# Index stage and even in-projection of a sparse-attention decoder put into one block, with the 256 best keys found by bisection

## The reference, cut to what matters

```python
def indexer_select(qi, wi, ki, qpos, topk):
    s = relu(einsum('bthd,bsd->bths', qi, ki))           # 8 heads of 64
    score = einsum('bths,bth->bts', s, wi)
    score = where(arange(L) <= qpos, score, -inf)
    _, idx = top_k(score, topk)                          # 256 of 1024; 136 of 544
...
def even_mixer(h, pos, R0, w_in, w_out, q_gain, k_gain, attend):
    qr, kr, vr, gr, qa, ka, va, qi, ki, wi = split(h @ w_in)
    ret, R = retention_branch(qr, kr, vr, gr, pos, R0)   # gate: silu(gr)
    qa, ka = rmsnorm(qa, q_gain), rmsnorm(ka, k_gain)
    att = attend(qa, ka, va, qi, ki, wi)
    return concatenate([ret, att], -1) @ w_out, R, ka, va, ki
```

## Time and profile before

| | |
|---|---|
| median of 3 runs | 3370.16 us (3369.79 to 3370.91) |
| span of the profiled execution | 3368.8 us |
| PE busy | 2930.4 us, 87% of the span |
| DVE busy | 1501.6 us, 45% |
| ACT busy | 683.3 us, 20% |
| POOL busy | 377.4 us, 11% |
| index stage, first to last | 65.15 to 278.9 us |
| even projection, to the next block | 278.9 to 646.8 us |

### The profile page before, as it was taken

How to read it: one execution, slowest core, us unless ns; L and a number is a source line. 1 busy time by engine, 2 the same in 40 slices (tenths; PEclk the granted TensorE clock), 3 DMA queues, 4 the chain that set the end, 5 groups by cost and what they waited for, 6 DMA issues and landing times. The chain is left out here.

```text
span 3368.8 us, 38811 instructions
## 1 busy us (share of the span) xinstructions
PE 2930.4 (87%) x16567; PEld 2680.5 (80%) x16567; DVE 1501.6 (45%) x2009; ACT 683.3 (20%) x1091; POOL 377.4 (11%) x352
## 2 busy tenths in 40 slices
PE   3397999772687989999999979977788999999998
PEld 3285777562563989999999979955488999999997
DVE  4058999477541342323323253436534323233233
ACT  2042111024331121111111122222132111111110
POOL 3602112250213010000000000005101000000000
PEclk6598999885798989999999989976698999999999
DMA  4002222304214121121211111100011111211111
GB/s 147 25 7 72 93 92 72 135 33 161 76 40 128 60 60 42 40 55 39 57 38 38 44 24 44 46 15 18 29 51 44 51 44 38 57 38 54 41 38 64
DMA packets 207072, 189.49 MB, mean 56 GB/s; under 512 B 18220, under 2 KB 159664, under 8 KB 206762
## 3 DMA queue, kind: packets, MB, share of 16 engines
q1 hardware_dynamic: 198321, 163.58, 16.1%
q0 software_dynamic: 8576, 23.34, 2.3%
HBM read 153.30 MB, written 33.50 MB: 55 GB/s over the span
## 5 line engine op out<-in xcount | busy, mean ns | idle before, releaser
L1877 DVE TENSOR_TENSOR xt<-ps,xt 128x1056 f32<-128x1056 f32 x176 | 221.1, 1256 | 207.1 <-PE ps L1661 207.1
L1661 PE MATMUL ps<-ffn_high,f_whG 128*128 128x352 f32 x1056 | 230.1, 326 | 13.2 <-DVE ffn_low L1591 7.8
L1661 PE MATMUL ps<-f_hidh,f_whD 128*128 128x352 f32 x1056 | 230.0, 326 | 9.9 <-DVE f_wlD L1856 9.9
L1661 PE MATMUL ps<-ffn_high,f_wlG 128*128 128x352 f32 x1056 | 227.4, 323 | 3.3 <-issue 3.3
L1661 PE MATMUL ps<-f_hidh,f_wlD 128*128 128x352 f32 x1056 | 229.7, 325 | 0.0
L1661 PE MATMUL ps<-f_hidl,f_whD 128*128 128x352 f32 x1056 | 228.8, 325 | 0.0
L1661 PE MATMUL ps<-ffn_low,f_whG 128*128 128x352 f32 x1056 | 228.7, 325 | 0.0
L1661 PE MATMUL ps<-ffn_low,f_whU 128*128 128x352 f32 x1056 | 228.7, 324 | 0.0
L1661 PE MATMUL ps<-ffn_high,f_whU 128*128 128x352 f32 x1056 | 227.8, 324 | 0.0
L1661 PE MATMUL ps<-ffn_high,f_wlU 128*128 128x352 f32 x1056 | 226.6, 323 | 0.0
L678 PE MATMUL ps<-pe_wh,even_high 128*128 128x512 f32 (+1 forms) x504 | 200.4, 398 | 11.7 <-POOL pe_wl L708 11.7
(11 more groups left out here) (534 smaller groups left out, 4878.3 us busy)
## 6 DMA issues: line engine op xcount, KB each, us to landing
pe_w<-in_w_in_even_dram SPq DMA_DIRECT2D x7, 2048.0 KB, 8.2
proj<-pe_out SPq DMA_DIRECT2D x56, 256.0 KB, 2.0
ht_even<-in_w_gate_dram SPq DMA_DIRECT2D x22, 512.0 KB, 5.3
ht_even<-in_w_up_dram SPq DMA_DIRECT2D x22, 512.0 KB, 6.5
ht_even<-in_w_down_dram SPq DMA_DIRECT2D x22, 512.0 KB, 3.9
ht_odd<-in_w_gate_dram SPq DMA_DIRECT2D x22, 512.0 KB, 5.1
ht_odd<-in_w_up_dram SPq DMA_DIRECT2D x22, 512.0 KB, 6.3
ht_odd<-in_w_down_dram SPq DMA_DIRECT2D x22, 512.0 KB, 3.9
```

What stands on the lines that cost most here:

```text
L1661: last = pe.matmul(g.ps[0:out_rows, b0 + c, 0:THIRD], lhs, rhs[:, c * THIRD:(c + 1) * THIRD], start=(first and n == 0), stop=(final and n ...
L1877: dve.tensor_tensor(xv, g.ps[:, 3 * (m % 2):3 * (m % 2) + 3, 0:THIRD], xv, ALU.add).then_inc(added, 1)
```

## The change

`stage_index` and `stage_project_even` become one block, `stage_mix_in`. What it does:

- **Order on PE.** The index projection comes first, then unit 0 of the even projection. From unit 1 to unit 24 two pairs of heads are scored in each unit, one after its fourth k and one at its end: 48 pairs, plain fp32 in one pass, with a head's 64 rows in the lower and the other head's in the upper half of the array. Cached pages are turned in units 28 to 35, sample tokens scored in 29 to 36, and summed in unit 38.
- **Weights** come in pieces of 128 x 512 through a ring of 4 raw and a ring of 12 split ones.
- **Gathers.** POOL issues 32 indirect DMAs instead of 64. They wait until all scores are weighted, then four follow each of the low parts 24 to 31.
- **Selection.** DVE finds, for the six tiles at once, the 256th largest score bit by bit: 32 passes, each with one count a tile (how many scores are at or above the candidate; L584) and two small instructions. Ties are then ranked and 10 more such passes find where to cut among them. After that come the sample tokens' 17 rounds of the old kind.
- **Moved to this block's ACT:** the Silu of the gate (with the copy of column block 3) and the squares of q and k (blocks 4 and 5).
- **Gone elsewhere:** tile 2's rounds, the Silu and the squares in retention and prep, and the sample's rounds in the prompt attention. In the prep, k and q are loaded and normed by thirds, and k is stored ahead of v.

```diff
+    UNITS = EVEN_TM * TILES
+    PAIRS = [(t, hp) for t in range(2, SMP) for hp in range(IH // 2)]
+    PER, PAIR_0 = 2, 1
...
+            def pair(p):                               # PE
+                t, hp = PAIRS[p]
+                if p >= 1:
+                    pe.wait_ge(rectified, 2 * p)
+                keys = (t + 1) * P
+                for c in range(-(-keys // 512)):
+                    hi = min(keys, (c + 1) * 512)
+                    for par in range(2):
+                        half = slice(ID * par, ID * par + ID)
+                        last = pe.matmul(g.ps[:, 4 + 2 * par + c, 0:hi - c * 512], qt[half, hp, t * P:(t + 1) * P],
+                                         kk[half, c * 512:hi], start=True, stop=True)
+                last.then_inc(scored, 1)
...
+            for n in range(3 * KD):                    # POOL
+                low(n)
+            pool.wait_ge(weighted, 2 * len(PAIRS))
+            pool.iota(rank, [[1, SEQ]], base=1, ...).then_inc(ranked, 1)
...
+            for n in range(3 * KD, EVEN_TM * KD):
+                low(n)
+                if n < 3 * KD + NB * NPAGE // 4:
+                    for p in range(4 * (n - 3 * KD), 4 * (n - 3 * KD) + 4):
+                        pool.indirect_dma_start(out=pages[:, p, :], ...).then_inc(pages_in, 16)
...
+            def count_all(threshold, op):              # DVE
+                for t in tiles:
+                    passes[0] += 1
+                    if passes[0] > 2:
+                        dve.wait_ge(counted, passes[0] - 2)
+                    dve.tensor_scalar(relu[:, passes[0] % 2, 0:(t + 1) * P], area(t), threshold[:, t - 2:t - 1], None,
+                                      op, ALU.add, accum_out=count[:, t - 2:t - 1]).then_inc(counted, 1)
+                dve.wait_ge(counted, passes[0])
+            for bit in range(MAX_BIT, -1, -1):
+                count_all(cand[:, :].bitcast(F32), ALU.is_ge)
+                link(dve.tensor_scalar(miss[:, :], count[:, :], float(TOPK), ..., ALU.is_lt, ALU.mult))
+                link(dve.scalar_tensor_tensor(out=cand[:, :], in0=cand[:, :], ..., in1=miss[:, :],
+                                              op0=ALU.bitwise_xor, op1=ALU.bitwise_xor))
...
+            dve.wait_ge(s_summed, 1)
+            link(dve.tensor_copy(g.score_s[:, 0:PAST], g.ps[0:NS, 7, :]))
...
+            choose(SMP, 0, rounds(SMP))
...
-            act.activation(gate[:, :, :], gate[:, :, :], ACT.Silu).then_inc(root_ready, 1)   # retention
-            choose(2, ROUNDS_2[0], ROUNDS_2[1])
...
-            choose(2, ROUNDS_2[2], ROUNDS_2[3])                                              # prep
-            link(dve.tensor_tensor(sv, kv, kv, ALU.mult))
-            link(dve.tensor_reduce(ms[:, 0, :], sv, AX.X, ALU.add))
+            for c, (lo, hi) in enumerate(THIRDS):
+                dve.wait_ge(k_in[c], 32 if hi == TILES else 16)
...
-                if FIRST <= n < FIRST + rounds(SMP):                                         # prompt attention
-                    choose(SMP, n - FIRST, n - FIRST + 1)
```

More of the change, by code:

```diff
@@ L1037, in _, with load @@
         def _(sp):
+            def load(buf, m, lo, hi, arrived):
+                full = min(hi, SMP)
+                sp.dma_start(buf[:, lo:full, :], g.proj[m, lo * P:full * P, :].rearrange("(c p) n -> p c n", p=P)
+                             ).then_inc(arrived, 16)
+                if hi == TILES:
+                    sp.dma_start(buf[0:NS, SMP, :], g.proj[m, SEQ:T, :]).then_inc(arrived, 16)
             with nc.allow_non_contiguous_dma("small tables"):
@@ L1051, in _ @@
                          ).then_inc(hank_in, 16)
-            sp.wait_ge(v_in, 32)
-            for buf, name, s in ((g.va, "v", None), (k, "k", normed_k)):
-                if s is not None:
-                    sp.wait_ge(s, 1)
+            sp.wait_ge(normed_k, 3)
+            for buf, name in ((k, "k"), (g.va, "v")):
+                if name == "v":
+                    sp.wait_ge(v_in, 32)
                 sp.dma_start(g.outs[f"{name}_prompt"][0, 0].rearrange("(c p) h d -> p c (h d)", p=P),
@@ L1064, in _ @@
         def _(pool):
-            for buf in (q, k, g.va):
+            for buf in (k, q, g.va):
                 pool.memset(buf[:, SMP, :], 0.0).then_inc(zeroed, 1)
@@ L1086, in _ @@
         def _(act):
+            act.wait_ge(rms, 1)
+            act.activation(g.ms[:, :, :], g.ms[:, :, :], ACT.Sqrt).then_inc(root, 1)
             act.wait_ge(bias_made, 1)
             act.copy(row[:, :], g.ps[0:H, 7, 0:384]).then_inc(bias_read, 1)
-            act.wait_ge(q_in, 32)
-            act.wait_ge(zeroed, 3)
-            for n in range(TILES * H):
-                t, h = n // H, n % H
-                act.activation(waste[:, :], q[:, t, h * P:(h + 1) * P], ACT.Square, accum_out=ms[:, 1, n:n + 1]
-                               ).then_inc(squared, 1)
-                act.wait_ge(squared, n + 1)
-            for n in range(2):
-                act.wait_ge(rms, n + 1)
-                act.activation(ms[:, n, :], ms[:, n, :], ACT.Sqrt).then_inc(root, 1)
             act.wait_ge(gain_ready, 1)
@@ L1113, in link, with heads @@
                 dve.wait_ge(chain, done[0])
-            dve.wait_ge(zeroed, 3)
+            def heads(buf, lo, hi):
+                return buf[:, lo:hi, :].rearrange("p t (h e) -> p (t h) e", h=H)
+            dve.tensor_scalar(g.ms[:, :, :], g.ms[:, :, :], 1.0 / P, EPS, ALU.mult, ALU.add).then_inc(rms, 1)
             dve.wait_ge(small_in, 48)
             dve.tensor_scalar(q_gain[:, :], q_gain[:, :], P ** -0.5, None, ALU.mult).then_inc(gain_ready, 1)
-            sv, kv = (x[:, :, :].rearrange("p t (h e) -> p (t h) e", h=H) for x in (sq, k))
@@ L1128, in _ @@
-            dve.wait_ge(root, 1)
-            link(dve.reciprocal(ms[:, 0, :], ms[:, 0, :]))
-            link(dve.tensor_tensor(kv, kv, spread(ms[:, 0, :], 1, P), ALU.mult))
-            dve.tensor_tensor(kv, kv, spread(k_gain[:, :], 0, TILES * H), ALU.mult).then_inc(normed_k, 1)
-            dve.wait_ge(root, 2)
-            link(dve.reciprocal(ms[:, 1, :], ms[:, 1, :]))
-            for t0 in range(0, TILES, 3):
-                part = q[:, t0:t0 + 3, :].rearrange("p t (h e) -> p (t h) e", h=H)
-                dve.tensor_tensor(part, part, spread(ms[:, 1, t0 * H:(t0 + 3) * H], 1, P), ALU.mult).then_inc(normed_q, 1)
@@ L1137, in _ @@
-            choose(2, ROUNDS_2[3], ROUNDS_2[4])
+            dve.wait_ge(zeroed, 3)
+            dve.wait_ge(root, 1)
+            link(dve.reciprocal(g.ms[:, :, :], g.ms[:, :, :]))
+            for c, (lo, hi) in enumerate(THIRDS):
+                dve.wait_ge(k_in[c], 32 if hi == TILES else 16)
+                part = heads(k, lo, hi)
+                link(dve.tensor_tensor(part, part, spread(g.ms[:, 1, lo * H:hi * H], 1, P), ALU.mult))
+                dve.tensor_tensor(part, part, spread(k_gain[:, :], 0, (hi - lo) * H), ALU.mult).then_inc(normed_k, 1)
@@ L1140, in page_slot @@
+            for c, (lo, hi) in enumerate(THIRDS):
+                dve.wait_ge(q_in[c], 32 if hi == TILES else 16)
+                part = heads(q, lo, hi)
+                dve.tensor_tensor(part, part, spread(g.ms[:, 0, lo * H:hi * H], 1, P), ALU.mult).then_inc(normed_q, 1)
 def page_slot(name, b):
```

754 lines of the change are left out of this document (401 added, 353 removed).

## The result

The changed kernel takes 3257.5 us (median of 4 runs, 3256.1 to 3258.7) against 3370.0 of the kernel before, measured beside it: a ratio of 0.967 (0.9656 to 0.9683), 112 us less. Forecast were 3310 us, with a range of 3275 to 3350.

The account below looks back on a forecast made before the run. PE bounds the two old blocks; in the merged block DVE's selection was to become the bound. From the 3368.8 us span, 23 for the block and 37 for later ones came off, plus 1.4 to the median: 3310 us, range 3275 to 3350.

Parts of the forecast that it names:

- Units 1 to 24 are 24 x 5.57 = 133.7: Merged block, PE: one 5.57 us projection unit each for units 1 to 24, 133.7 us before E.
- E: Time of the last score in the merged block, where DVE's selection chain starts; forecast at 315.5 us.
- DVE becomes the bound, by some 38 us: Merged block: DVE's selection, formerly hidden under PE's projection, ends the block at 623.5; PE ends at 581 plus 3.
- counts at L629's rate: Rival: a count pass takes 3.9 us, DVE 86 us shorter, PE the bound at 584; 3270 us; chance 0.08.
- Two halves work side by side: Pairs' matmuls overlap in the array halves, 28.4 us instead of 56.8; in turn is the rival, 3338 us, chance 0.23.
- the 10 us that were put in: Pairs on PE: some 96 changes between full and half array with their waits, 0.1 each, 10 us (0 to 20).
- the slower rival: PE at 1.2 GHz through units 1 to 24, pauses at each pair keeping it there; 3472 us; chance 0.06.
- A pass: One bisection pass of DVE's selection: 5.55 us of counts plus 0.4 of small operations, 5.95; 42 passes 250.
- Gathers: Merged block, after E: 32 gathers starve engines of issue, 5 us added to DVE's chain (0 to 28).
- Retention: Retention: 5.03 us wait for the Silu goes, sample loop gives 1 to 2, table load may appear: 6 us gained.
- Prep: Prep stage: without rounds and squares the transfers bound it, ending at 825; a gain of 21 us (17 to 27).
- Prompt attention: Prompt attention: without the rounds, 17 x 0.85 us is 14 at most; taken as 10 gained (7 to 14).

Follow-up runs that it names:

- The run without ties: The changed kernel without the 10 passes that find where to cut among equal scores; 3262.1 us, ratio 0.969.
- the run without the stall: The changed kernel with four gathers behind each of low parts 24 to 27 and 32 to 35, pages turned from unit 34; 3244.3 us, ratio 0.962.
- the row behind low part 31: The changed kernel with all 32 gathers in a row behind low part 31, pages turned from unit 34 instead of 28; 3274.1 us, ratio 0.972.

## Why the prediction was wrong

**The step that failed** is "Units 1 to 24 are 24 x 5.57 = 133.7". There are 12 such units, so E came 67 us too late by this term. Measured E is 252.7, 63 before the forecast. The other terms of E held: the index projection was forecast to end at 132.9 (the first copy out of its last block is at 133.94), unit 1 to start at 143.4 (142.6), and the pairs to cost 38.4. From 142.6 to the end of the last pair at 248.9 are 106.3, and less 12 x 5.57 this leaves 39.4. That the place of the pairs explains E and most of the time is shown by the kernel with one pair a unit: E is 316.3 there, and the time 3306.7 against 3310 forecast.

**The bound.** "DVE becomes the bound, by some 38 us" was E + 308 (302, 5 and 1) against E + 269 for PE with its last store. PE has 50 units left behind unit 12, not 38; in the prediction's own terms these are 50 x 5.57 + 15 + 3 = 296.5, so the count alone still leaves DVE last, by 12 us. That PE ends 13 us after DVE instead comes of smaller terms: DVE took 298 us after E, and PE 311, because unit 27 waits for low parts and its clock falls. The prediction had these low parts and gathers done 50 us after E, which is ahead of unit 27 once 12 units are counted; in the profile they start 41 us after E (293.48), and the last four low parts come only behind 326.24. The run without ties shows that PE ends the changed kernel's block; in the run without the stall PE's end is 12.8 us earlier, level with DVE's in the changed kernel, and DVE ends last. The rival "counts at L629's rate" at 3270 came closest to the time for a reason that is false: counts do go at L1284's rate.

**What was right.**
- The index projection is free of its gaps without gathers beside it; that gathers cause them is confirmed by adding 32 (20 us).
- Two halves work side by side: 1.92 against 3.20 us for a pair. The rest of a pair is right in sum only. A pair of 1024 keys takes 2.13 us beyond the projection's own 2.78, of which 1.72 are 4 x 0.86 / 2; the other 0.4, in each of 24 pairs, is the 10 us that were put in as 0.1 for each of 96 changes, where there are 48. The Trainium skill's rule that a change of array mode drains the engine ("TensorEngine Tiling (Array Packing)", "Key Properties") would fit these 0.4 us. That the drain is their cause was not tried.
- Pairs don't stall PE: it was busy 105.96 of 106 us from 143 to 249 at a granted clock of 0.98, so the slower rival is out. It waits for relus once, 2.0 us behind the last pair.
- The counts' rate: the form that writes its accumulator took 1275 ns at 1024 elements. The threshold that is read from a tile is not what costs: L617 in the changed kernel, the plain form with such a threshold, took 747 ns. The Trainium skill ("SBUF — State Buffer", "Who interferes with whom") leaves the form that writes out its accumulator off its list of operations that can enter the two-port modes, and the trace agrees: 1275 ns against L629's 695.

**Sizes that were off.**
- A pass is 5.73 us where nothing disturbs it, not 5.95, since five of the six accumulator reads are hidden. But the small operations of some passes take up to 1.2 us instead of 0.17, so the 42 passes took 248 us, against 250 forecast. The long ones run beside POOL's low parts (L591 at 372.51 for 1.20 us, a low part at 372.39 for 1.30); whether these are the cause was not tried.
- Gathers: 0 instead of 5 us of starved issue; they stand in fours with a low part between, not in a row. PE's stall at unit 27, whose place was named, is 9.8 us of waiting and a granted clock of 0.75 from 331 to 358.
- Retention: 0 instead of 6. The tail is shorter as forecast, by 3.7: DVE no longer waits for the Silu, but the square root's table has to be loaded there (ACT's timeline):

```profile
693.23 1.28 ACT L1054 ACT_TABLE_LOAD   x1 [16.47 <-DVE rt_ms L1111]
```

  The rest of the stage took it back. Its sample loop and the scoring ahead of it, 662.2 to 688.6, are 26.4 us against 24.9 for the same 136 matmuls at a granted clock of 0.69 against 0.75, and the chunks ahead of them 95.7 against 93.2 at 0.73 against 0.76 (stretches of the changed kernel, then of the one before):

```profile
566.50:662.20 95.70, 50.82 (x328) 47.51 (x328) 68.13 (x99) 20.07 (x77) 61.01 (x69) 0.73 0.34 121
662.20:688.60 26.40, 24.16 (x136) 20.12 (x136) 6.48 (x11) 2.71 (x14) 9.29 (x6) 0.69 0.02 7
```

```profile
646.80:740.00 93.20, 48.78 (x328) 45.26 (x328) 78.92 (x123) 20.28 (x78) 60.32 (x69) 0.76 0.36 125
740.00:764.90 24.90, 21.99 (x136) 19.16 (x136) 15.01 (x35) 2.50 (x13) 9.30 (x6) 0.75 0.02 5
```

  Why the clock is lower was not tried and stays open.
- Prep: 21 as forecast.
- Prompt attention: 3.2 instead of 10. Units at the step from one query tile to the next, starts on DVE:

```profile
795.02 0.29 DVE L1400 COPY ht_even<-ps 128x128 f32<-128x128 f32 x1 [0.69 <-PE ps L1334]
797.32 0.29 DVE L1400 COPY ht_even<-ps 128x128 f32<-128x128 f32 x1 [0.62 <-PE ps L1334]
799.96 0.29 DVE L1400 COPY ht_even<-ps 128x128 f32<-128x128 f32 x1 [0.96 <-PE ps L1334]
802.82 0.29 DVE L1400 COPY ht_even<-ps 128x128 f32<-128x128 f32 x1 [1.18 <-PE ps L1334]
```

  The units of the next tile take 2.86 us by PE alone. The step from 2.30 to 3.15 in the earlier trace rows, which the estimate multiplied by 17, was a step between tiles as much as the round's: without the rounds this unit takes 2.64. In the first tile behind the step 0.4 to 0.5 us a unit went, in the next 0.15 to 0.4, and from a pitch of 3.95 on nothing.
- Later layers: 7.9 us less with no line changed. From the sample attention's L1489 (L1393 before) to the end are 2320.5 us before and 2312.6 after. In the eight experiments the same stretch is 2312.8 to 2316.5. Part of it may be the scatter between executions, which for the kernel before was 3363 to 3378 us beside the experiments; there is one profile of the kernel before, and it is not settled.

With 12 units in place of 24 and every other term as it was written, E is 248.7, PE ends at 248.7 + 50 x 5.57 + 15 + 3 = 545 and DVE at 248.7 + 302 + 5 + 1 = 557, and the forecast is 3370.2 - 90 - 37 = 3243 us, 14 below the measured time. Of that, 10 are in the block (567 against 557), by PE's stall at unit 27; in the version without the stall the next block opens at 556.6. Retention and the prompt attention lack 13 more, and the later layers give 8 of it back: the 37 us forecast behind the block come out as 32, but 8 of these from layers that the prediction did not name, which is luck.

## What to carry to other kernels

Count a loop's trips from its bounds and set the count against the row that it must end on before it is priced: one factor of two in a count moved the end of the chain by 67 us. It also shrank the margin by which DVE was to end last from 39 us to 12, and a stall that the sum no longer had then made PE the last. Where a chain of one engine starts when another is partly done, both ends have to be summed from that same point, with all the work that is then left on each, and with what frees the buffers on the way. Gathers that POOL issues in one unbroken row can keep the other engines from issuing; put other work of POOL between every few of them, and keep them away from operands that another engine is about to want.

## What the runs showed of the hardware

- Indirect DMAs of 128 rows in an unbroken row, 1.26 us apart, left PE at pace for 18 to 24 us (14 to 18 gathers) and then held it to one matmul in some 2.8 us, in three places: the old index projection, the 32 added ones, and the row behind low part 31. DVE showed waits for issue too in the first and the last of them.
- Fours of gathers with one low part of 1.3 us between held nobody from issuing. They needed no longer pause: with one pair a unit all 32 go so from 319.4 to 367.7, and DVE is busy 48.17 us of the 49 from 331 to 380, with no wait for issue (PE waits for low parts there, 25.9 us in all, so its own need was low). Why so little between is enough was not tried.

```profile
331.00:380.00 49.00, 24.89 (x78) 16.69 (x79) 48.17 (x113) 5.18 (x8) 31.43 (x31) 0.62 0.23 67
```

- Plain fp32 matmuls over 64 rows each ran beside each other in the two halves of the array (eight instructions of 512 columns in 1.92 us, 3.20 on one half), also when both of one half stood ahead of both of the other (1.92).
- On DVE the accumulator read of a count and the next count start together (256.95 both, behind a count of 0.61 us that began at 256.41), so the read costs nothing there; the last read of a pass, at 261.61, is waited for (L591 at 261.73).
